# The mixer's operands cut in row form and turned by transposing DMAs in place of TensorE, and the last gate's product in banks of its own

## The reference

```
u   = rmsnorm(x) @ w_in                      # (tokens, 10256), split into q, k, v, gates, ...
y_a = (rmsnorm(o_a) * silu(gg)) @ w_gla      # o_a: gated linear attention, 1024 wide
y_b = (o_b * silu(dg)) @ w_dil               # o_b: three dilated windows merged, 512 wide
merged = sigmoid(ga) * y_a + sigmoid(gb) * y_b
h   = x + rmsnorm(merged @ w_out) * g_post
out = h + (pe @ w_ple_proj) * sigmoid(h @ w_ple_gate)    # pe: 256 wide
```

## Time and profile before

| | us |
|---|---|
| median of 3 runs | 3044.16 (3041.31 to 3045.29) |
| the profiled execution's own time | 3046.62 |
| its span in the profile | 3044.8 |
| TensorE busy | 2982.5 of the span |
| mixer, from its first product (2297.92) to the end | 747 |

### The profile page before, as it was taken

How to read it: one execution, slowest core, us unless ns; L and a number is a source line. 1 busy time by engine, 2 the same in 40 slices (tenths; PEclk the granted TensorE clock), 3 DMA queues, 4 the chain that set the end, 5 groups by cost and what they waited for, 6 DMA issues and landing times.

```text
span 3044.8 us, 44599 instructions
## 1 busy us (share of the span) xinstructions
PE 2982.5 (98%) x17982; PEld 1633.4 (54%) x17982; DVE 1018.4 (33%) x2419; ACT 904.2 (30%) x1968; POOL 346.3 (11%) x573
## 2 busy tenths in 40 slices
PE   6999999999999999999999999999998999999998
PEld 3544456666545665666456555555544445454443
DVE  4211134444333442433133311211213544445432
ACT  4201124443313332333133212222213444344431
POOL 0000010100220102210001022222000000000000
PEclk9999999999999999999999999999999999999999
DMA  5234354555565656564659476666356232222310
GB/s 194 88 111 145 119 176 140 183 191 175 200 230 202 175 183 217 193 199 137 200 186 321 128 263 243 227 218 217 115 187 233 105 111 105 101 100 101 115 47 18
DMA packets 159605, 502.24 MB, mean 165 GB/s; under 512 B 21677, under 2 KB 26613, under 8 KB 156953
## 3 DMA queue, kind: packets, MB, share of 16 engines
q1 hardware_dynamic: 111674, 256.91, 25.0%
q0 software_dynamic: 47728, 242.49, 23.5%
HBM read 361.74 MB, written 236.67 MB: 197 GB/s over the span
## 4 chain that ended last, share of the span: by engine, by line
PE 95%; DMA 3%; DVE 1%; ACT 1%; issue 0%; POOL 0%; SPq 0%; POOLq 0%; DVEq 0%; ACTq 0%
PE out L2286 53%; PE out L1898 21%; PE out L1048 2%; PE out L1033 2%; PE out L1871 2%; PE out L2289 2%; PE out L1243 2%; PE out L1039 1%; PE out L549 1%; PE out L1257 1%; PE out L559 1%; PE out L560 1%; PE out L1277 1%; PE out L1025 1%; PE out L1026 1%; PE out L288 1%
## 5 line engine op out<-in xcount | busy, mean ns | idle before, releaser
L2286 PE MATMUL out<-w_hi,xn_hi 128*128 128x512 f16 x2560 | 974.6, 381 | 2.0 <-DVE w_lo L2174 2.0
L2286 PE MATMUL out<-w_lo,xn_hi 128*128 128x512 f16 x2560 | 973.4, 380 | 0.0
L2286 PE MATMUL out<-w_hi,xn_lo 128*128 128x512 f16 x2560 | 973.0, 380 | 0.0
L2286 PEld LDWEIGHTS out<-w_hi,xn_lo 128*128 128x128 f16 x2560 | 251.2, 98 | 304.1 <-issue 3.7
L2286 PEld LDWEIGHTS out<-w_hi,xn_hi 128*128 128x128 f16 x2560 | 251.5, 98 | 281.2 <-issue 18.0
L2286 PEld LDWEIGHTS out<-w_lo,xn_hi 128*128 128x128 f16 x2560 | 251.3, 98 | 266.0 <-issue 2.7
L2202 ACT ACTIVATE stage<-out 128x512 f32<-128x512 f32 (+1 forms) x170 | 99.3, 584 | 879.0 <-PE out L2286 841.1
L2234 DVE TENSOR_SCALAR stage<-out 128x512 f32<-128x512 f32 (+1 forms) x170 | 114.7, 675 | 640.4 <-PE out L2286 610.6
L1078 DVE CUSTOM_DVE_ANT_0 score<-out,mask 128x128 f32<-128x128 f32 (+1 forms) x192 | 70.0, 365 | 316.8 <-PE out L1033 303.6
L1057 ACT ACTIVATE qT<-out 128x128 f32<-128x128 f32 x192 | 53.0, 276 | 352.1 <-PE out L1026 351.9
L2174 DVE SCALAR_TENSOR_TENSOR w_lo<-raw,w_hi 128x1024 f16<-128x1024 f32 x80 | 97.5, 1221 | 129.8 <-ACT w_hi L2168 129.6
(11 more groups left out here) (308 smaller groups left out, 3920.5 us busy)
## 6 DMA issues: line engine op xcount, KB each, us to landing
U<-stage SPq DMA_DIRECT2D x320, 256.0 KB, 3.0
out<-in_cache_kv_w POOLq DMA_DIRECT2D x64, 1020.0 KB, 8.8
raw<-in_w_in SPq DMA_DIRECT2D x80, 512.0 KB, 4.4
sw_kc<-in_cache_kv_w POOLq DMA_DIRECT2D x24, 1024.0 KB, 6.4
sw_vc<-in_cache_kv_w POOLq DMA_DIRECT2D x24, 1024.0 KB, 10.2
out<-in_cache_kv_w POOLq DMA_DIRECT2D x16, 1008.0 KB, 7.5
mix_og<-OG SPq DMA_DIRECT2D x16, 780.0 KB, 4.3
OG<-result POOLq DMA_DIRECT2D x8, 1040.0 KB, 12.8
```

The lines of the kernel that those rows point to most:

```text
L2286: last = pe.matmul(out[m % 3][:, :], x[:, k, at:at + P], y[:, k, :], start=first, stop=final)
```

## The change

- The operands are cut into halves while tokens are still on the partitions: ScalarE copies z, pe, m and h from SBUF to float16 rows (`z_row`, `pe_row`, `m_row`, `h_row`), VectorE subtracts these from the float32 rows.
- SyncE then issues eight transposing DMAs a turn, SBUF to SBUF (`turn_pe`, `turn_z`, `turn_m`, `turn_h`, one each for hi and lo), and TensorE waits for their semaphores. The 30 transposes by TensorE, the two PSUM banks `T` and `self.chunk` are gone.
- gate writes to the two banks that `T` had, now called `G`; `A` belongs to gla alone.
- On TensorE a turn is gla, dil, out, gate, proj without a break. On ScalarE and VectorE the halves of m(t) come right behind merge(t), those of z(t+1) and pe(t+1) behind make_z(t+1), those of h(t-1) behind add_out(t-1).
- `g_post` is loaded at the head of `queue_weights` in place of much earlier, and sits in other memory; three slots of turned pe in place of four.

```diff
-        self.T, self.A, self.B, self.C = bank[3:5], bank[5:7], [bank[7], bank[0]], bank[1:3]
+        self.G, self.A, self.B, self.C = bank[3:5], bank[5:7], [bank[7], bank[0]], bank[1:3]
...
+    def turn_z(self, sp, t):
+
+        rows = self.rows(t)
+        after(sp, self.z_lo, 3 * (t + 1))
+        after(sp, self.y_made, t)
+        for part in range(2):
+            sp.dma_start_transpose(self.zT[part][:, :, :rows], self.z_row[part][:rows, :]).then_inc(self.z_turned.sem, 16)
+
+    def turn_pe(self, sp, t):
+        rows = self.rows(t)
+        after(sp, self.z_lo, 3 * (t + 1))
+        after(sp, self.proj_made, t - 2)
...
+    def turn_m(self, sp, t):
+        rows = self.rows(t)
+        after(sp, self.m_lo, t + 1)
+        after(sp, self.out_made, t)
...
+    def turn_h(self, sp, t):
+        rows = self.rows(t)
+        after(sp, self.h_lo, t + 1)
+        after(sp, self.gate_made, t)
...
         if slot == self.TURN_SLOT + 6:
-            after(sp, self.turned, self.chunk["z", 0, 3] + 1)
+            self.turn_z(sp, 0)
             self.load_early(sp, 1)
 
     def queue_weights(self, sp):
+        sp.dma_start(self.g_post_sb[:, :], self.g_post.to_broadcast([P, D_MODEL])).then_inc(self.g_loaded.sem, 16)
...
         if self.has(t):
+            self.turn_pe(sp, t)
             self.load_x(sp, t)
         if self.has(t + 1):
             after(sp, self.merged, t + 1)
-            if t >= 1:
-                after(sp, self.turned, self.chunk["m", t - 1, 1] + 1)
+            after(sp, self.m_lo, t)
             self.load_gates(sp, t + 1)
+            self.turn_z(sp, t + 1)
         if self.has(t + 2):
-            after(sp, self.turned, self.chunk["z", t + 1, 3] + 1)
             self.load_early(sp, t + 2)
+        if self.has(t):
+            self.turn_m(sp, t)
+        if self.has(t - 1):
+            self.turn_h(sp, t - 1)
...
+    def z_hi_half(self, act, t):
+        rows = self.rows(t)
+        after(act, self.z_ready, t + 1)
+        after(act, self.z_turned, t * 32)
+        act.activation(self.z_row[0][:rows, :GLA_VAL], self.oa[:rows, :, :].rearrange("p h c -> p (h c)"), ACT.Copy).then_inc(self.z_hi.sem, 1)
...
+    def m_lo_half(self, dve, t):
+        rows = self.rows(t)
+        after(dve, self.m_hi, t + 1)
+        dve.tensor_tensor(self.m_row[1][:rows, :], self.ga[t % 2][:rows, :], self.m_row[0][:rows, :], ALU.subtract).then_inc(self.m_lo.sem, 1)
...
     def tensor(self, pe, t):
         rows = self.rows
         if self.has(t):
-            after(pe, self.lo_ready, self.chunk["z", t, 1] + 1)
-            after(pe, self.gate_ready, (t - 2) * 2)
+            after(pe, self.z_turned, (t + 1) * 32)
+            after(pe, self.products_gated, t)
             self.product(pe, self.A, self.zT, "gla", rows(t))
...
         if self.has(t - 1):
-            after(pe, self.lo_ready, self.chunk["m", t - 1, 1] + 1)
+            after(pe, self.m_turned, t * 32)
             after(pe, self.out_scaled, t - 1)
             self.product(pe, self.C, self.mT, "out", rows(t - 1)).then_inc(self.out_made.sem, 1)
...
+            after(pe, self.h_turned, (t - 1) * 32)
+            after(pe, self.gate_ready, (t - 2) * 2)
+            self.product(pe, self.G, self.hT, "gate", rows(t - 2)).then_inc(self.gate_made.sem, 1)
```

More of the change, by code:

```diff
@@ L1635, in pool, with m_hi_half, h_hi_half @@
             self.norm_m(pool, t - 1)
[L1639 to L1649, removed]
+    def z_hi_half(self, act, t):
[3 more added lines that the diff above has]
+        act.activation(self.z_row[0][:rows, :GLA_VAL], self.oa[:rows, :, :].rearrange("p h c -> p (h c)"), ACT.Copy).then_inc(self.z_hi.sem, 1)
+        act.activation(self.z_row[0][:rows, GLA_VAL:], self.dg[:rows, :, :].rearrange("p h c -> p (h c)"), ACT.Copy).then_inc(self.z_hi.sem, 1)
+        after(act, self.pe_turned, t * 32)
+        act.activation(self.pe_row[0][:rows, :], self.pe_in[:rows, :], ACT.Copy).then_inc(self.z_hi.sem, 1)
+    def m_hi_half(self, act, t):
+        rows = self.rows(t)
+        after(act, self.merged, t + 1)
+        after(act, self.m_turned, t * 32)
+        act.activation(self.m_row[0][:rows, :], self.ga[t % 2][:rows, :], ACT.Copy).then_inc(self.m_hi.sem, 1)
+    def h_hi_half(self, act, t):
+        rows = self.rows(t)
+        after(act, self.h_ready, t + 1)
+        after(act, self.h_turned, t * 32)
+        act.activation(self.h_row[0][:rows, :], self.x[t % 3][:rows, :], ACT.Copy).then_inc(self.h_hi.sem, 1)
     def ask(self, act, t):
@@ L1697, in scalar_before @@
         if slot == self.TURN_SLOT:
-            for n in range(4):
-                self.keep_hi(act, "z", 0, n, self.kept("z", 0, n, 0))
+            self.z_hi_half(act, 0)
     def scalar(self, act, t):
@@ L1707, in scalar @@
             self.square_a(act, t + 1)
[L1708 to L1712 removed]
         if self.has(t + 1):
             self.silu(act, t + 1)
[L1715 to L1718 removed]
+        if self.has(t):
+            self.m_hi_half(act, t)
@@ L1734, in keep_lo, with z_lo_half @@
-    def keep_lo(self, dve, stage, t, n):
-        c, rows = self.chunk[stage, t, n], self.rows(t)
-        out, half = self.kept(stage, t, n, 1), self.kept(stage, t, n, 0)
-        after(dve, self.hi_ready, c + 1)
-        blocks = out.shape[1]
-        dve.tensor_tensor(out[:, :, :rows], self.T[c % 2][:, :blocks * P].rearrange("p (n t) -> p n t", t=P)[:, :, :rows], half[:, :, :rows],
-                          ALU.subtract).then_inc(self.lo_ready.sem, 1)
+    def z_lo_half(self, dve, t):
+        rows = self.rows(t)
+        for i, (part, whole) in enumerate(((slice(0, GLA_VAL), self.oa), (slice(GLA_VAL, GLA_VAL + WIDTH), self.dg))):
+            after(dve, self.z_hi, 3 * t + i + 1)
+            dve.tensor_tensor(self.z_row[1][:rows, part], whole[:rows, :, :].rearrange("p h c -> p (h c)"), self.z_row[0][:rows, part],
+                              ALU.subtract).then_inc(self.z_lo.sem, 1)
+        after(dve, self.z_hi, 3 * t + 3)
+        dve.tensor_tensor(self.pe_row[1][:rows, :], self.pe_in[:rows, :], self.pe_row[0][:rows, :], ALU.subtract).then_inc(self.z_lo.sem, 1)
@@ L1836, in vector_before @@
         if slot == self.TURN_SLOT:
-            for n in range(4):
-                self.keep_lo(dve, "z", 0, n)
+            self.z_lo_half(dve, 0)
     def vector(self, dve, t):
```

126 lines of the change are left out of this document (41 added, 85 removed).

## The result

The changed kernel takes 3000.3 us (median of 4 runs, 2996.36 to 3000.82) where the kernel before, run beside it, takes 3043.4 (3041.31 to 3045.29): ratio 0.9853, 95% interval 0.9839 to 0.9868, so 1.5% faster. The forecast was 2995 with a range of 2984 to 3036; for the profiled execution it was 2997.8, and that took 2.6 more.

A forecast was written before the change was run, and what follows sets the result against it. TensorE, busy 98% of the span, was taken as the bound. Terms of -41.7, -2.4, -2.9, +9.1, -5.8 and -5.1 sum to -48.8 us, from 3046.62 to 2997.8; the forecast median was 2995, range 2984 to 3036.

The forecast's parts named there:

- turn 0's transposes in the projection: Before the mixer: turn 0's 8 transposes amid the projection go, with their waits, 2.9 us less.
- start, gla of turn 0 to gla of turn 3: Mixer start: TensorE waits for z of tiles 1 and 2, then runs at slower clock; 112.8 us for 103.7, cost 9.1.
- turns 3 to 15: Thirteen steady turns: without TensorE's transposes each takes 38.86 us for 42.1, 41.7 us less in all.
- turn 16: Turn 16, 41.3 us before, falls to 38.86 without its transposes: 2.4 us less.
- turn 17: Turn 17, 29.1 us with transposes and waits, becomes out, gate and proj alone, 23.3: 5.8 us less.
- turn 18: Last gate: transposes and wait of 3.3 us and slow clock of 1.9 go, 5.1 us less.
- z comes in time: Steady turn: z's last halves are ready 27.2 us in, leaving 11.7 us for its transposes, so TensorE does not wait.
- X: Time from z's last half to both its transposes landed, taken as 6 us.
- The bounds: Limits on z's transpose time: 4.7 us from a plain transfer of its size, 7.0 from twice the runs of `og`.
- Rival (3): Mixer start: SyncE held by pe's transposes behind 9 MB of weights, 2998 us; no clock drop, 2991; chance 0.70 with the forecast.
- The last turn: End: last h turned 11.5 us after out, while gate and proj of the tile before take 12.95, so no wait.
- The other things to see: Profile signs: period 38.9 us, no z wait, eight issues, idle about 21 and 7 us, no wait before last gate.

The follow-up runs named there:

- experiment 1: Kernel before the change with every transpose of the mixer by TensorE issued twice: 3093.7 us, ratio 1.0153 to the kernel before.
- (3): Changed kernel with z's two transposing DMAs issued behind the five loads, not ahead of them: 3020.0 us, ratio 0.9917 to the kernel before.
- (4): Changed kernel with z's transposes issued behind the five loads and m's transposes: 3075.0 us, ratio 1.0107 to the kernel before.
- experiment 5: Changed kernel with pe's transposes of tile 0 right behind z's and the weights of gate and proj queued behind turn 0's work: 2994.4 us, ratio 0.9845.
- experiment 7: Changed kernel with the last tile's h turned into z's memory in place of `hT`: 2993.4 us in one execution.
- experiments 9 and 10: 9: changed kernel, z ahead of merge, gate/proj weights queued in turn 1, last h in own memory, 2975.6 us; 10: also z turned in two parts, 2980.7 us.

## Why the prediction was right

| term | forecast | measured |
|---|---|---|
| turn 0's transposes in the projection | -2.9 | -1.88 |
| start, gla of turn 0 to gla of turn 3 | +9.1 | +9.04 |
| turns 3 to 15 | -41.7 | -42.41 |
| turn 16 | -2.4 | -2.06 |
| turn 17 | -5.8 | -5.50 |
| turn 18 | -5.1 | -3.49 |
| sum | -48.8 | -46.30 |

The terms are differences between starts of products (before, of the transposes ahead of them) in the two profiles; the ends of the spans differ by 46.3. The 2.5 us between the two sums are the first term and the last. The other 2.5 or so by which 3000.3 lies above 2995 are the step from the profiled execution to the median: the forecast took 2.5 off for it, as before, and after the change the two are the same (3000.38 and 3000.3).

**The steady turns.** Right in mechanism and size. Thirteen turns went from 547.55 us (2401.42 to 2948.97) to 505.14; experiment 1 shows that the 3.27 us a turn were the transposes' own.

**z comes in time.** X was 5.6 for 6. The room was 11.5 for 11.7: at 12.9 a turn waits (3), at 13.4 and more all do and the kernel is slower (4). The bounds came from plain transfers. The unit of 256 bytes in the upper one (7.0) is right: of the 96,996 packets under 512 B from 2420 to 2900 us 92,160 have 256 bytes, and 30 blocks of 128 rows in two halves, 7,680 a turn, are that number in 12 turns. But what it was measured against is wrong: the trace before shows no runs of 520 bytes, `og` goes in packets of 6240, 128 to a load. The 3,072 runs of z are not twice those of `og` but 24 times, so that bound had no ground, and that 6, taken between it and 4.7, came so near is in part luck. The lower bound, by bytes, holds. The Trainium skill's 261 GB/s for a DMA transpose ("DMA: Bandwidth & Descriptors", Latency and other measured facts), 1.5 us for each half of z beside a fixed part, is not at odds with 3.8 and 4.1 us to landing, of which no row tells the fixed part.

**The rule that spoke against it.** z's two issues took SyncE 1.27 + 1.96 = 3.2 us. By the Trainium skill's table of cycles ("DMA: Bandwidth & Descriptors", section "Why a DMA increments its semaphore by 16 and not by 1") I had estimated 5.1: too high here. But behind other traffic an issue takes longer: m's two, right behind the five loads, 2.96 + 4.70 us, h's 1.25 + 1.34 at once after them. The turn's total (1.27 + 1.96 + 2.96 + 4.70 + 1.25 + 1.34 + 1.47 + 1.25 = 16.2) is above the 12.8 of the estimate, and so is the sum of the medians of all turns, 14.4 (m's are 2.1 and 3.9), for another reason than the number of tiles: m and h have equally many.

**The start.** The sum was right and its parts were not, as far as the first wait goes. Forecast: halves 11.7 us after dil, transposes landed 9.5 later. Measured: z's issues begin 14.7 us after dil (2326.36 - 2311.63) and gla starts 6.1 after that. 20.8 for 21.2: two errors of some 3 us that cancel, which is luck. What I had missed is that z's issue waits for pe's halves, these for `pe_row` of tile 0, and that for transposes queued behind the weights (3.8 us of ScalarE's idle time; 3.0 of the 3.5 us of experiment 5). What I had overpriced is the queue: by 2326 the weights were through, so z's transposes took 6.1. Rival (3) gave 3 us to pe's transposes behind the weights, but by another way, SyncE held. SyncE was held, 7.26 us, but it was free again at 2312.5 and waited for the merge, and later for the halves; the memory of `pe_row` was what kept z back. Gla of turn 2 came at 70.9 for 72.0, gla of turn 3 at 112.6 for 112.8, with slow clock after each wait: 1.5 us in turn 1 (27.41 for 25.9, 0.2 of which is the last matmul's own end) and 2.9 in turn 2 (41.76 for 38.86), 4.4 in all for 3.8 forecast.

**Turn 0's transposes.** The mixer's first product starts 1.9 us earlier than in the profile before. In eleven profiles of kernels that are alike up to there it starts between 2291.4 and 2298.2 (median 2295.4). One profile of before can't tell 1.9 from 2.9, so whether this term is right stays open.

**The last turn.** This step failed: h would be turned 11.5 us after out, gate and proj take 12.95, so no wait. The halves were as early as forecast, 8.2 us after out (2963.3). The operand was ready at 2971.5, but `hT` is one buffer, and gate of tile 15 reads it until 2973.84. The transposes, 3.9 us with their issue, can't be done before 2977.8, 1.5 us after proj. I had read when the operand is ready and not when its memory is free; experiment 7 gives it other memory, and the wait is gone. Of the 1.6 us by which this term is short, 1.5 are this wait.

**The other things to see.** No wait in the steady turns, eight issues a turn, about 21 and 7 us of idle time at the start: all as the text said. No z transpose took over 5 us (the longest took 4.74). The wait before the last gate is the one sign that came out otherwise.

## What to carry to other kernels

Moving work off a full engine was worth its own time there and no more; whether the replacement is late is a question of room, and the room could be found from the engines' order in the profile of before to 0.2 us. When an operand is now delivered by DMA, ask for each transfer when its source is ready, when its destination is free, and what stands ahead of it in its queue: the first was right here in every place, the second failed at the end, the third at the start. After such a change look at the start and the end of the loop, where the skew leaves nothing to hide a wait: here 22 us more lay in the order of a few issues and helper instructions and in one destination, nearly half of what the change itself brought.

## What the runs showed of the hardware that was not expected

- The issue of a transposing DMA takes SyncE longer behind queued loads: 7.26 us for the second half of pe (128x256 only) behind the 9 MB of weights, 10.13 and 9.36 us for h behind 5 MB in experiments 9 and 10, 2.96 and 4.70 for m behind 2188 KB. In turn 15, which has none of the five loads, m's two take 1.46 and 1.35 us, and pe's and h's take 1.2 to 1.5 in nearly all turns. A plain load in the same place (`mix_x`, `mix_gb`) took 1.77 and 3.30 us. SyncE issues nothing else in that time.
- With no large loads right ahead of them, pe's transposes landed 2.4 to 3.0 us after issue in the median, h's 3.2 to 3.3, z's 3.8 to 4.1, for 128x256, 128x1024 and 128x1536; six times the elements took 1.3 to 1.7 times as long, so by an estimate from these times some 2 us or more of each are a fixed part.
- Eight transposes a turn brought the DMA engines' busy share from 0.29 to 0.62 and slowed TensorE's matmuls by nothing (busy in 505.14 of 505.14 us at a granted clock of 1.00, and 38.86 a turn, which is what the products took before). The loads beside them went from 4.3 to 5.2 us to landing (`og`).
- A wait can cost clock as well. The granted clock of the first stretch was 0.86 in the mean, of full speed (2.4 GHz): it fell to 1.2 GHz in both waits and was still there when TensorE went on.

```profile
2332.50:2360.00 27.50, 27.36 (x120) 11.99 (x120) 12.89 (x27) 11.32 (x20) 1.27 (x2) 0.95 0.55 161
2367.00:2406.00 39.00, 39.00 (x169) 17.02 (x168) 19.13 (x34) 16.19 (x26) 2.50 (x6) 0.93 0.64 169
```

- Five hundredths of 27.5 us are 1.4, seven of 39 are 2.7: about what turns 1 and 2 lost (1.3 without the last matmul's end, and 2.9), after 20.8 and 7.0 us of idle time. So the longer wait did not cost more. In experiment 4, with waits of 2.3 to 4.5 us, nine of twelve turns lost some 1.7 us and three (after 2.8, 2.6 and 2.3 us) nothing. The wait of 1.5 us before the last gate cost no clock: the 60 matmuls take 13.15 us at a granted clock of 1.00, and as much in experiment 7, where no wait stands ahead of them. The 12.95 of the earlier trace rows, by which I had priced the clock at 1.9 us, is a part of a longer piece; against 13.15 it is 1.7.
